# Two attentions: scores of two heads at once in the array's row halves, a step earlier, exponentials in place

## What is computed

```python
# banded: chunks of 64 queries, 8 chunks of keys to the left and their own
s = einsum('bqhd,bkhd->bhqk', qc, kc) * scale + bias      # a bias per head and distance
ya = softmax(s) @ vc  * silu(ga)                          # keys and values of each head
# sparse: one key and one value head for all 8 query heads
score = sum_h relu(iq_h . ik) * iw_h                      # selects 256 keys per query
yb = softmax(q @ k_selected * scale) @ v_selected * silu(gb)
```

## Time and profile before

| | |
|---|---|
| median of 3 runs | 4560.41 us |
| the profiled execution, first to last instruction | 4557.4 us |
| PE (TensorE) busy | 4225.0 us, 93% |
| PEld (weight loads) busy | 2573.4 us, 56% |
| VectorE (DVE) busy | 2646.4 us, 58% |
| ScalarE (ACT) busy | 1410.5 us, 31% |
| GpSimd (POOL) busy | 734.0 us, 16% |
| HBM traffic over the span | 199 GB/s |

### The profile page before, as it was taken

How to read it: one execution, slowest core, us unless ns; L and a number is a source line. 1 busy time by engine, 2 the same in 40 slices (tenths; PEclk the granted TensorE clock), 3 DMA queues, 4 the chain that set the end, 5 groups by cost and what they waited for, 6 DMA issues and landing times. The chain is left out here.

```text
span 4557.4 us, 62056 instructions
## 1 busy us (share of the span) xinstructions
PE 4225.0 (93%) x22261; PEld 2573.4 (56%) x22261; DVE 2646.4 (58%) x6147; ACT 1410.5 (31%) x2889; POOL 734.0 (16%) x750
## 2 busy tenths in 40 slices
PE   7899999999976999979889999999979979998998
PEld 6656566565642333335456454545447768777765
DVE  4544444434344333336468999999966655556665
ACT  1233323333320111113357301010137767661000
POOL 0011110100103555532142000000012121000000
PEclk9899999999987999989989999999989989999999
DMA  9765655556415878746473544544463242113331
GB/s 293 240 194 160 195 144 180 167 171 176 149 55 207 320 239 294 249 149 210 146 195 103 164 122 111 152 111 117 131 188 94 66 100 74 53 59 118 111 120 61
DMA packets 661912, 705.33 MB, mean 155 GB/s; under 512 B 195928, under 2 KB 514608, under 8 KB 648688
## 3 DMA queue, kind: packets, MB, share of 16 engines
q1 hardware_dynamic: 570192, 495.68, 36.4%
q0 software_dynamic: 63696, 185.05, 12.0%
q10 hardware_dynamic: 27728, 20.71, 1.4%
HBM read 770.36 MB, written 135.36 MB: 199 GB/s over the span
## 5 line engine op out<-in xcount | busy, mean ns | idle before, releaser
L2004 PE MATMUL l_unit<-l_xT,l_w 128*128 128x512 f32 x2048 | 912.3, 595 | 32.7 <-DMA l_xT<-mid_xn3T 29.1
L2004 PEld LDWEIGHTS l_unit<-l_xT,l_w 128*128 128x128 f32 x2048 | 388.3, 191 | 471.3 <-issue 458.9
L2105 DVE TENSOR_SCALAR_CACHE_REDUCE l_work<-l_score,l_trial 128x384 bf16<-128x384 f32 (+1 forms) x434 | 617.3, 1476 | 8.9
L430 PE MATMUL f_ring<-f_win,f_hT 128*128 128x512 f32 x1024 | 462.9, 608 | 15.2 <-issue 8.6
L1370 PE MATMUL e_ph<-e_gateup,e_rowsT 128*64 128x512 f32 x1536 | 343.9, 601 | 6.7 <-DVE e_rowsT L1537 5.0
L430 PEld LDWEIGHTS f_ring<-f_win,f_hT 128*128 128x128 f32 x1024 | 194.7, 194 | 254.7 <-issue 241.9
L2475 DVE CUSTOM_DVE_ANT_0 sparse_scores<-sparse_s,sparse_pen 128x512 f32<-128x512 f32 (+3 forms) x320 | 182.8, 609 | 180.8 <-PE sparse_s L126 163.9
L538 PE MATMUL f_ring<-f_wout,f_trio 128*128 128x512 f32 x512 | 226.7, 601 | 1.4 <-DVE f_trio L921 1.4
L1370 PEld LDWEIGHTS e_ph<-e_gateup,e_rowsT 128*64 128x64 f32 x1536 | 108.6, 138 | 206.1 <-issue 200.8
L1551 DVE TENSOR_TENSOR e_act<-e_ph,e_sig 128x256 f32<-128x256 f32 x48 | 20.4, 425 | 343.8 <-ACT e_sig L1417 343.8
L1680 PE MATMUL b_pp<-entry_w,b_xT 128*128 128x424 f32 (+1 forms) x512 | 208.0, 560 | 2.3 <-DVE b_xT L1782 2.3
(11 more groups left out here) (425 smaller groups left out, 7195.6 us busy)
## 6 DMA issues: line engine op xcount, KB each, us to landing
f_win<-in_w_in SPq DMA_DIRECT2D x64, 2048.0 KB, 8.2
l_w<-in_w_in SPq DMA_DIRECT2D x144, 512.0 KB
f_win<-in_w_in SPq DMA_DIRECT2D x128, 256.0 KB, 5.0
mid_ys<-e_out SPq DMA_DIRECT2D x48, 512.0 KB
f_wout<-in_w_ada SPq DMA_DIRECT2D x20, 1024.0 KB, 12.1
f_win<-in_w_in SPq DMA_DIRECT2D x16, 1024.0 KB, 7.0
mid_gzT<-l_out SPq DMA_DIRECT2D x64, 256.0 KB
o_gates<-mid_gzT SPq DMA_DIRECT2D x16, 1024.0 KB, 9.5
```

Source lines behind the costliest of these rows:

```text
L430: mm = nc.tensor.matmul(to[:, :], hT[:, k, :], w[:, k, :], start=(k == 0), stop=(k == KD - 1))
L2004: mm = nc.tensor.matmul(pu[n % 2][:, :], w[:, n % WB, k, :], xT[:, t % 2, k, :], start=(k == 0), stop=(k == KD - 1))
L2105: V.tensor_scalar(unread, score(b), at_least(b), None, op, ALU.add, accum_out=count[:, b:b + 1])
```

## The change

Queries and keys are no longer split. Heads 2p and 2p + 1 lie in partitions 0 to 63 and 64 to 127 (in the sparse attention the one key head lies in both), and `scores(i, p, c)` forms both heads' chunk as two fp32 products of 64 rows into two of the three banks, with one `qk` count for the two. POOL has nothing to do in these stages; ScalarE copies only group 0 of the banded keys into place; keys of groups 1 to 3 are loaded straight into their place, all at the stage's start, the values with them. Scores and row maxima run two steps ahead, exponentials one. VectorE writes the scores to a ring of six rows of probabilities, where ScalarE takes the exponentials in place, the first head's behind the evacuations of chunk 0, the second's behind those of chunk 1. All scores of a later step stand between the chunks of the present one. `gated` is cut in two, and its first part, `scale_gate`, goes ahead of the row maxima. Loads of queries take all 128 partitions in one transfer.

```diff
@@ -1896,10 +1896,9 @@
                     sp.wait_ge(dot, len(DOTS))
                     for u in range(OB):
                         sp.wait_ge(stored[u], 16 * 2)
-                    for part in range(2):
-                        sp.dma_start(g.band_q[part * HD:(part + 1) * HD, 0, :, :], g.qa2T.rearrange("(h d) t -> d h t", d=HD)[:, :, 0:P]).then_inc(g.band_q_loaded, 16)
-                        sp.dma_start(g.band_raw[part * HD:(part + 1) * HD, :, :],
-                                     g.ka2T.rearrange("(h d) t -> d h t", d=HD)[:, :, LEFT * CW:LEFT * CW + 512]).then_inc(g.band_raw_loaded, 16)
+                    sp.dma_start(g.band_q[:, 0, 0:AH // 2, :], g.qa2T.rearrange("(c p) t -> p c t", p=P)[:, :, 0:P]).then_inc(g.band_q_loaded, 16)
+                    sp.dma_start(g.band_raw[:, 0:AH // 2, :],
+                                 g.ka2T.rearrange("(c p) t -> p c t", p=P)[:, :, LEFT * CW:LEFT * CW + 512]).then_inc(g.band_raw_loaded, 16)
...
-
...
+    AHEAD = 2
+    SB, TB, RING = 3, 3, 6
+    GROUPS = T // 512
+
+    def piece(i, p, c, m):
 
         return first[i] + 2 * (p * len(WIDTHS[i]) + c) + m
...
-        q = g.band_q if banded else sb("q", [P, 2, NH, P])
-        q_parts = [sb(f"q_{part}", [P, 2, NH, P]) for part in ("head", "rest")]
-        raw = g.band_raw if banded else sb("k_raw", [P, RAW, PIECE])
-        kk = sb("k", [P, KH, T])
...
-        S = sb("scores", [P, 2, KW])
-        Pb = sb("probs", [P, PB, KW])
+        S = sb("probs", [P, RING, KW])
         PT = sb("probsT", [P, 4, 512])
-        mx = sb("max", [P, 2, 8])
+        mx = sb("max", [P, RING, 8])
...
-                def load_k(grp, h):
...
+                def load_k(grp):
+                    cols = slice(grp * 512, (grp + 1) * 512)
+                    if banded:
+                        sp.dma_start(kk[:, :, cols], by_pairs(g.ka2T)[:, :, pad + grp * 512:pad + (grp + 1) * 512]).then_inc(k_loaded[grp], 16)
+                    else:
+                        for m in range(2):
+                            sp.dma_start(kk[half(m), 0, cols], g.kbT[:, cols]).then_inc(k_loaded[grp], 16)
...
                     u, cols = i % 2, slice(i * P, (i + 1) * P)
                     if i >= 2:
-                        sp.wait_ge(q_ready, i - 1)
-                    for part in range(0 if banded and i == 0 else 2):
-                        sp.dma_start(q[part * HD:(part + 1) * HD, u, :, :], (g.qa2T if banded else g.qbT).rearrange("(h d) t -> d h t", d=HD)[:, :, cols]).then_inc(q_loaded[u], 16)
+                        sp.wait_ge(qk, first[i - 1] // 2)
+                    if not (banded and i == 0):
+                        sp.dma_start(q[:, u, :, :], by_pairs(g.qa2T if banded else g.qbT)[:, :, cols]).then_inc(q_loaded[u], 16)
...
+                load_q(0)
                 if not banded:
-                    load_q(0)
-                    load_k(0, 0)
+                    load_k(0)
                 load_v(0)
-                if banded:
-                    load_q(0)
                 load_q(1)
-                if not banded:
-                    for grp in range(1, 4):
-                        load_v(grp)
-                for i in range(NB):
-                    for grp, h in k_prep(i):
-                        load_k(grp, h)
-                    if banded and i < 3:
-                        load_v(i + 1)
-                    if i + 2 < NB:
-                        load_q(i + 2)
+                for grp in range(1, GROUPS):
+                    load_k(grp)
+                    load_v(grp)
+                for i in range(2, NB):
+                    load_q(i)
...
-            @block.gpsimd
...
-                    head(nc.gpsimd, q_parts[0][:, u, :, :], q[:, u, :, :])
-                    pool.drain()
-                    rest(nc.gpsimd, q_parts[1][:, u, :, :], q[:, u, :, :], q_parts[0][:, u, :, :]).then_inc(q_ready, 1)
...
+                def scores(i, p, c):
+                    n = piece(i, p, c, 0)
+                    if p == 0 and c == 0:
+                        if banded and i == 0:
+                            pe.wait_ge(g.band_q_loaded, 16)
+                        else:
+                            pe.wait_ge(q_loaded[i % 2], 16 * (i // 2 + (0 if banded and i % 2 == 0 else 1)))
+                        if i % 4 == 0 and not (banded and i == 0):
+                            pe.wait_ge(k_loaded[i // 4], 16 if banded else 32)
+                    if banded and i == 0 and c == 0:
+                        pe.wait_ge(first_ready, p + 1)
+                    if n + 1 >= SB:
+                        pe.wait_ge(s_read, n + 1 - SB + 1)
                     w = WIDTHS[i][c]
                     at = P * (i + 1 - TILES[i]) + 512 * c
-                    keys = kk[:, h if banded else 0, at:at + w]
-                    one_pass(nc, bs[n % SB][:, 0:w], q_parts[0][:, i % 2, h, :], keys, start=True, stop=False)
-                    one_pass(nc, bs[n % SB][:, 0:w], q_parts[1][:, i % 2, h, :], keys, start=False, stop=True).then_inc(qk, 1)
+                    for m in range(2):
+                        mm = nc.tensor.matmul(bs[(n + m) % SB][:, 0:w], q[half(m), i % 2, p, :], kk[half(m), p if banded else 0, at:at + w], start=True, stop=True)
+                    mm.then_inc(qk, 1)
...
-                for m in range(2):
-                    for c in range(len(WIDTHS[0])):
-                        scores(0, m, c)
-                for (i, p), ahead in zip(STEPS, STEPS[1:] + [None]):
+                for i, p in STEPS[0:AHEAD]:
+                    for c in range(len(WIDTHS[i])):
+                        scores(i, p, c)
+                for s, (i, p) in enumerate(STEPS):
                     nch = len(WIDTHS[i])
-                    later = []
-                    if ahead:
-                        ni, np_ = ahead
-                        for c in range(len(WIDTHS[ni])):
-                            scores(ni, 2 * np_, c)
-                        later = list(range(len(WIDTHS[ni])))
+                    ahead = step_at(s + AHEAD)
+                    later = len(WIDTHS[ahead[0]]) if ahead else 0
                     for c in range(nch):
                         turn(i, p, c, 0)
                         turn(i, p, c, 1)
                         if i and p == c == 0:
                             inverse_rows(i - 1)
-                        for n in later[2 * c:2 * c + 2] if c + 1 < nch else later[2 * c:]:
-                            scores(ni, 2 * np_ + 1, n)
+                        for n in range(later * c // nch, later * (c + 1) // nch):
+                            scores(*ahead, n)
                         if c:
                             values(i, p, c - 1)
...
-                def split_k(grp, h):
-                    n = KH * grp + h
-                    if banded and grp == 0:
-                        act.wait_ge(g.band_raw_loaded, 32)
-                    else:
-                        act.wait_ge(raw_loaded[n % RAW], 32 * (n // RAW + (0 if banded else 1)))
-                    nc.scalar.activation(kk[:, h, grp * PIECE:(grp + 1) * PIECE].bitcast(F32R), raw[:, n % RAW, :], ACT.Copy).then_inc(k_head, 1)
+                def first_keys(p):
+                    if p == 0:
+                        act.wait_ge(g.band_raw_loaded, 16)
+                    nc.scalar.activation(kk[:, p, 0:512], g.band_raw[:, p, :], ACT.Copy).then_inc(first_ready, 1)
 
                 def probs(i, h):
-                    act.wait_ge(m_ready, NH * i + h + 1)
-                    if h >= PB:
-                        act.wait_ge(tp, turned(i, (h - PB) // 2, len(WIDTHS[i]) - 1, 1) + 1)
-                    elif i:
-                        act.wait_ge(tp, turned(i - 1, (h + PB) // 2, len(WIDTHS[i - 1]) - 1, 1) + 1)
-                    keys = P * TILES[i]
-                    nc.scalar.activation(Pb[:, h % PB, 0:keys], S[:, h % 2, 0:keys], ACT.Exp, bias=mx[:, h % 2, 7:8],
+                    n, keys = NH * i + h, P * TILES[i]
+                    act.wait_ge(m_ready, n + 1)
+                    nc.scalar.activation(S[:, n % RING, 0:keys], S[:, n % RING, 0:keys], ACT.Exp, bias=mx[:, n % RING, 7:8],
...
-                for h in range(KH):
-                    split_k(0, h)
+                if banded:
+                    for p in range(PAIRS):
+                        first_keys(p)
                 probs(0, 0)
                 probs(0, 1)
-                for (i, p), ahead in zip(STEPS, STEPS[1:] + [None]):
+                for s, (i, p) in enumerate(STEPS):
                     nch = len(WIDTHS[i])
+                    ahead = step_at(s + 1)
                     for c in range(nch):
                         evacuate(i, p, c, 0)
                         evacuate(i, p, c, 1)
-                        if ahead and c == min(1, nch - 1):
-                            probs(ahead[0], 2 * ahead[1])
-                        if ahead and c == min(2, nch - 1):
-                            probs(ahead[0], 2 * ahead[1] + 1)
-                    for grp, h in k_prep(i)[p - 1:p] if p else ():
```

(63 more changed lines are left out.)

91 lines of the change are left out of this document (19 added, 72 removed).

## The result

The changed kernel takes 4575.85 us (median; 4572.0 to 4578.8), the kernel before 4560.66 beside it: ratio 1.0033, interval 1.0022 to 1.0045. It is 15 us slower, where 20 us faster was forecast. The profiled execution spans 4577.0 us against 4557.4.

The account below looks back on a forecast made before the run. PE's written order was taken to bound the long stretches, but not the first blocks. Banded +3 and sparse -24 gave -21 on the 4557.4 us span, 4536; with the median 3 above the span, 4540 us, range 4505 to 4580.

Parts of the forecast that it names:

- prices on PE: PE costs read from the earlier trace: transpose 0.109 us, turn 0.15, turn into halves 0.095, both heads' 512 keys 0.86.
- sparse 4 to 11: Sparse attention, blocks 4 to 11: 214.5 us forecast against 212, so +3.
- the 0.65 of the earlier trace: First stage's scores of 64 rows: eight records of 128 columns with the turn out, taken as showing halves overlap.
- the bank wait: Late banded steps: PE waits 0.63 us for a score bank before the 128-column scores; bounds 0 and 1.09.
- rival (a): Row halves overlap only in part at 512 columns, making the kernel slower: 4600 us, without any overlap near 4665; chance 0.13.
- 0.52: Sparse step of 15 tiles: PE's wait near its end for the last evacuation behind an exponential, forecast to go.
- the queries of banded block 2: Banded start: PE wants these loads at 3385, gets them near 3396 and waits 11 us, at 300 GB/s.
- Rival (b): The burst of loads decides: at 152 GB/s PE idles some 38 us, +25, 4562 us, no change; chance 0.15.
- banded blocks 0 to 3: Banded attention's first blocks: -7 us beside the start; bounds -18 with no wait for loads, +20 at 152 GB/s.
- the inverse rows in late banded blocks: Banded blocks 4 to 15: once a block 4 inverse-row transposes, 0.44 us, and about 0.5 of wait for them.
- sparse blocks 0 to 3: Sparse attention's first blocks: two steps ahead the chain has slack, ScalarE comes next; 45 us against 51, -6.
- (c): No bank wait and fast loads: -21 -30 -7, 4500 us; chance 0.10.

Follow-up runs that it names:

- run 1: Changed kernel with each call of scores issuing its two row-half products twice into the same banks; 4745.9 us in one run.
- run 3: Changed kernel with four score banks and two transpose banks instead of three and three, in both attentions; 4552.9 us, ratio 0.998.
- run 4: Changed kernel with loads of blocks 2 and 3 issued behind the second group of keys and values, not all four; 4570.5 us, ratio 1.0023.
- run 5: Changed kernel with VectorE's gated product of the block before placed ahead of the row maxima, in both attentions; 4573.4 us, ratio 1.0029.
- run 2: Kernel before with the changed kernel's schedule, scores still full-array products from split queries and keys; 4532.6 us, ratio 0.9935.
- run 9: run 7 with ScalarE's issue of the transfer of y moved to the end of a block's second step, both attentions; 4500.6 us, ratio 0.9872.
- run 11: run 9 plus grouped sparse values, but sparse scores in row halves too, without splits, three score and three transpose banks; 4521.5 us, ratio 0.9927.
- run 7: Changed kernel, banded with four score banks, calls in twos, early loads; sparse scores full-array from splits, as in run 2; 4513.2 us, ratio 0.9896.

## Why the prediction was wrong

- **The failed step is a term of the prices on PE**: that the turn into halves costs 0.095 and "a score record of 512 columns covers" the rest. From short records I saw that something falls between the first and second product behind a turn, and argued it away for wide ones. It is not covered: 0.106 at 512 columns and 0.101 at 128 (run 1), in 272 calls, 29 us. About 10 of them lie in banded 4 to 15, 9 in sparse 4 to 11, 6 in 12 to 15. The term was in the trace of before: the 0.65 of the earlier trace rows is 0.214 to the second pair of records, twice 0.112, and 0.208 to the next shape. I compared only its total with 0.86.
- **A second term was missing**: two calls in one chunk slot where the count of chunks grows. Eight steps have two, 1.2 to 1.3 each (run 3), 10 us: 5 of the 16 that sparse 4 to 11 missed, and 2.5 in either attention's block 3.
- *Right:* the bank wait (0.63 forecast, 0.64 measured; 46 waits in all); overlapping halves, so rival (a) is false; 0.20 from the last transpose to the first score; no wait before the last sparse values,'s 0.52 being gone. A sparse step of 15 tiles is 11.63, which is 11.20 and four times 0.106, and a banded one 4.76, which is 4.53 and twice 0.106.
- *Luck:* the estimate under rival (a), 1.12 a pair of halves and 4575 us, is as good as the measured 4575.9, and a call does hold PE for 1.06. But its cause, halves that overlap only in part, is not there: the second call of run 1 takes 0.86, what full overlap gives.
- *Right in kind, small in effect:* the queries of banded block 2. PE waited 4.3 (forecast 11) until 3395.3 (forecast 3396), at 308 GB/s (forecast 300) in 3366 to 3390. Rival (b) is out by that and by run 4. That banded blocks 0 to 3 gained 4.4 of the forecast 7 is in part luck: the wait was 6.7 shorter than forecast, and what took it back was in no term (the 0.106, the double calls, and the second steps' wait below).
- *Too much:* 0.5 a block for the inverse rows in late banded blocks. Their wait isn't there: the block's first step is 0.43 longer, four transposes. That hid some 6 us of the missing term.
- *Wrong in sign:* sparse blocks 0 to 3, 9.0 above the forecast. The second steps of blocks 2 and 3 were to take 2.7 and 3.15 and took 3.91 and 4.39, as good as before (4.00, 4.38). The chain has slack, as argued, but ScalarE's in-order transfer of y waits there for the gated product behind the row maxima, 6.9 us in two waits (before, one of 1.3), and with the product earlier (run 5) the two steps lose 2.7. Block 3 has its double calls, 2.5, and the 0.106 of 16 calls makes 1.7; the last 2 I can't place. Banded blocks 2 and 3 waited in the same way.
- *Slips in the rivals' sums, on which nothing hangs:* an idle time of 38 in place of 11 is +27, not +25, so (b) would be 4567; by the bounds given, fast loads in (c) are worth 11, not 7.
- *Left open:* what of run 2's 29 us comes from the scores two steps ahead and what from the earlier exponentials; neither was tried alone. Nor was the banded attention run on the full array with run 9's later store, early loads and four banks, so what its row halves are worth in the best order (3.91 a late step, against 4.10 in run 2) isn't known. What the 0.106 is rests on the load records of run 1 and isn't tested by a run of its own. "TensorE: Matmul & The Clock Gate" of the Trainium skill, Part 2, Step-by-step, says that the next weights load while the current product runs. The trace agrees: within a call each load starts with the product before its own, and the loads that stand exposed are those first behind a turn (0.107 for the scores, 0.058 for the transposes).

## What to carry to other kernels

Count the turns between shapes of the array, not only the products. Here a call in row halves between transposes costs 0.30 us beyond its streaming and 0.28 more than the same scores on the full array, 0.13 more where values follow. Row halves did worse in the sparse attention (run 11); joining two calls behind one turn gives 0.21 back for each, and without splits the first scores start some 3 us earlier. Behind a turn look at the second record's distance, and don't expect a wider product to cover it. Count, too, how many score banks a call takes at once (four in place of three gave 23 us here), and look at the steps where loop counts change, where an even interleave puts two calls in one slot. Compare stages, not only spans, when a gain is a few us. And before a change of several parts is dropped, run its parts: here the schedule was worth -29 us and the row halves, with their bank waits, +45.

## What the runs showed of the hardware

- The first fp32 product behind a turn into row halves shows its second record late, by 0.106 us at 512 columns (0.533 for 0.427) and 0.101 at 128 (0.213 for 0.112); later products of the same call don't (run 1).
- Its second weight load starts 0.107 after its first and the second product 0.427 after that; later loads start with the product before their own (run 1, 3561.18 to 3562.15). So the first load behind the turn is the one that shows.
- From the last full-array transpose to the first score is 0.202 in row halves. To full-array scores it is 0.028, but their second record comes 0.319 after the first in place of 0.231 (run 2, 3602.647, 3602.675, 3602.994): together 0.347, and 0.109 and 0.231 would be 0.340, so no turn shows.
- The two row halves start 7 ns apart and overlap in full: a second call of 512 columns, two records in each half, takes 0.86 (run 1).
- A transfer that ScalarE issues in order, and that waits for VectorE, holds up that engine's evictions: 1.83 us in run 7's second steps, and 0.57 of each of these steps on PE (4.49 against 3.92 in run 9).
